# In the up pass, the gate groups of two tiles are run together, three in a row, behind the second tile

## The reference

```python
q  = (xt @ wq).reshape(t, 8, 2, 128)
s  = einsum('thpc,pnc->thpn', q, subkeys)      # 128 keys on each side
sv, si = top_k(s, 16)                          # 16 best on each side
cand   = sv[:, :, 0, :, None] + sv[:, :, 1, None, :]
cv, ci = top_k(cand, 16)                       # 16 of 256 pairs
eidx   = ia * 128 + ib                         # one of 16384 experts
gate   = softmax(cv)
hc  = gelu(einsum('chkd,cd->chk', u[eidx], x)) # up
out = einsum('chk,chkd->cd', hc * gate, v[eidx]) # down
```

## Time and profile before

| | |
|---|---|
| median of 3 runs | 3200.64 us (3191.85 to 3200.99) |
| the profiled execution | 3202.49 us, of which the span is 3200.7 us |
| PE busy | 3069.8 us, 96% of the span |
| DVE, POOL, ACT busy | 2551.4, 1746.1, 1382.4 us |
| DMA | 920.92 MB, mean 288 GB/s |
| matmuls of the up tiles (L1637), both layers | 6144 records |
| matmuls of the gate groups (L1669) | 1536 records, 192 groups |
| matmuls of the down pass (L1689) | 4608 records |

### The profile page before, as it was taken

The page is one execution under the profiler, slowest core; times in us unless marked ns, Lnnn a source line. Parts: engine busy times, 40 slices in busy tenths (PEclk is TensorE's granted clock), DMA queues, the critical chain, the costliest instruction groups (busy, mean ns, idle before and its releaser), DMA issues.

```text
span 3200.7 us, 46734 instructions
## 1 busy us (share of the span) xinstructions
PE 3069.8 (96%) x17222; PEld 2780.8 (87%) x17222; DVE 2551.4 (80%) x4953; ACT 1382.4 (43%) x2559; POOL 1746.1 (55%) x1160
## 2 busy tenths in 40 slices
PE   7879999999999999999888889999999999999997
PEld 7879999999998888888685789999999988888886
DVE  7755999977775999999567358989877759999987
ACT  2522343477764333333344223343777653333332
POOL 4543488887775444443130223788877755544442
PEclk9989999999999999999887899999999999999998
DMA  3212499999999999999130022799999999999993
GB/s 106 77 53 91 128 340 337 339 397 393 393 392 373 401 400 399 401 397 351 53 95 1 27 67 80 274 348 342 371 400 387 395 370 394 399 401 400 398 400 138
DMA packets 286579, 920.92 MB, mean 288 GB/s; under 512 B 27344, under 2 KB 77392, under 8 KB 282688
## 3 DMA queue, kind: packets, MB, share of 16 engines
q1 hardware_dynamic: 154336, 415.63, 35.9%
q0 software_dynamic: 111280, 404.77, 33.4%
q10 hardware_dynamic: 20736, 97.53, 7.4%
HBM read 817.34 MB, written 102.38 MB: 287 GB/s over the span
## 4 chain that ended last, share of the span: by engine, by line
PE 77%; DVE 16%; DMA 3%; POOL 2%; issue 1%; ACT 1%; DVEq 0%; ACTq 0%; SPq 0%
PE ps L1689 34%; PE ps L1637 22%; PE ps L1563 11%; PE ps L1669 5%; POOL low L604 2%; DMA raw<-uT 1%; PE ps L1811 1%; DVE xn L948 1%; DVE xl L941 1%; DVE cand L1218 1%; DVE cand L1225 1%; DVE slot L1231 1%; PE ps L1765 1%; PE ps L1800 1%; DVE rowsB L1129 1%
## 5 line engine op out<-in xcount | busy, mean ns | idle before, releaser
L762 ACT ACTIVATE high<-raw 128x1024 fp32r<-128x1024 f32 x512 | 542.7, 1060 | 992.2 <-PE ps L1689 665.9
L1637 PE MATMUL ps<-xh,high 128*128 128x384 f32 x2048 | 699.1, 341 | 14.8 <-POOL low L604 14.6
L604 POOL TENSOR_TENSOR low<-raw,high 128x1024 fp32r<-128x1024 f32 x256 | 614.2, 2399 | 167.2 <-ACT high L762 160.5
L1637 PE MATMUL ps<-xh,low 128*128 128x384 f32 x2048 | 687.4, 336 | 0.0
L1637 PE MATMUL ps<-xl,high 128*128 128x384 f32 x2048 | 686.2, 335 | 0.0
L1689 PE MATMUL ps<-high,hh 128*128 128x512 f32 x1536 | 483.5, 395 | 7.9 <-DVE low L1301 7.9
L1689 PE MATMUL ps<-low,hh 128*128 128x512 f32 x1536 | 481.1, 394 | 0.0
L1689 PE MATMUL ps<-high,hl 128*128 128x512 f32 x1536 | 480.3, 393 | 0.0
L595 POOL DMA_INDIRECT rowsA<-v,pick x192 | 271.3, 1413 | 296.9 <-DVE ps L1136 288.8
L1637 PEld LDWEIGHTS ps<-xh,high 128*128 128x128 f32 x2048 | 386.1, 189 | 20.8 <-POOL low L604 19.8
L595 POOL DMA_INDIRECT rowsB<-v,pick x192 | 240.2, 1251 | 271.0 <-DVE ps L1136 255.6
(11 more groups left out here) (279 smaller groups left out, 5043.5 us busy)
## 6 DMA issues: line engine op xcount, KB each, us to landing
raw<-uT SPq DMA_DIRECT2D x256, 512.0 KB
raw<-v SPq DMA_DIRECT2D x256, 512.0 KB
gate_dram<-gblk ACTq DMA_DIRECT2D x24, 2048.0 KB
gt<-gate_dram SPq DMA_DIRECT2D x32, 1536.0 KB
s_dram<-sring ACTq DMA_DIRECT2D x120, 384.0 KB
sring<-s_dram SPq DMA_DIRECT2D x120, 384.0 KB
raw<-wts SPq DMA_DIRECT2D x74, 512.0 KB, 3.6
rowsB<-u,pick POOLq DMA_INDIRECT x192
```

The costliest lines, as they stand in the source:

```text
L604: pool.tensor_tensor(low[:, m % 4], raw[:, m % 4], high[:, (m + 2) % 3].bitcast(F32), ALU.subtract).then_inc(sem("lo_ready"), 1)
L762: act.activation(high[:, (m + 2) % 3], tile_raw(m), ACT.Copy).then_inc(sem("hi_ready"), 1)
L1637: ins = pe.matmul(ps[:, m % 2, 0:DN], w[:, c], x[:, c, 0:DN], start=(c == 0 and k == 0), stop=(c == NC - 1 and k == 2))
```

## The change

`groups_of` gives nothing for an even tile, and for an odd tile m what the old one gave for m-1 and m together.

```diff
 def groups_of(m):
 
-    lo = min(int(max(0, m - GROUP0) * GROUPS_PER_TILE), DN // 4)
+    if m % 2 == 0:
+        m -= 1
+        lo = hi = min(int(max(0, m + 1 - GROUP0) * GROUPS_PER_TILE), DN // 4)
+        return range(lo, hi)
+    lo = min(int(max(0, m - 1 - GROUP0) * GROUPS_PER_TILE), DN // 4)
     hi = min(int(max(0, m + 1 - GROUP0) * GROUPS_PER_TILE), DN // 4)
     return range(lo, hi)
```

## The result

The changed kernel takes 3236.2 us (median of 4, 3231.01 to 3240.3) beside 3200.81 before: ratio 1.0109 (95% interval 1.0088 to 1.013), 35 us slower. Timed once more, it was 1.0103 (1.0085 to 1.0121). Forecast were +14 us and at most 3232. The direction was right, and the pause of PE at the third group is there; but it is larger than I made it, and something that I had put "under cover" costs 9 us beside the 17 of the pause.

The account below looks back on a forecast made before the run. PE was taken to set the pace. Bank pause 10.5 + ACT's small gelu and slot copy 1 + uT loads 1.5 + late store 1 - switches 0 = +14 us, giving 3214.5 us, range 3198 to 3232.

Parts of the forecast that it names:

- under cover: POOL's low halves and gathers, DVE's one-hots and SP's loads in the gate stretch: shifted but hidden, 0 us.
- what is removed: One switch between tile and groups and back per pair, 32 a layer: at most 0.01 us each, taken as 0.
- The bound of 5 us: Most that saved switches could give, if the slower first matmul step after a group (0.25 against 0.17) were a price.
- The pause: PE waits before each row's third group for ScalarE's copy to free the bank: 0.17 us a row, 10.5 us total.
- The rule of the Trainium skill: Rotate groups through banks; by it alone a group (0.89) outlasts a copy (0.58), so two banks lose nothing.
- the 1.5 us for them: ACT's waits for uT loads reaching the next row: perhaps three a layer by 0.3 us, 1.5 to 2 us.
- the 1 us for tiles 64 and 68: Small gelu and slot copy in front of high_tile at m = 64 and 68: 0.5 us a layer, 1 us.
- Rival 2: ACT's lateness from uT loads runs from row to row and reaches PE: 3240 us, chance 0.12.
- The sign of being wrong that I had named: No idle time before third groups, or idle in front of a tile ended by POOL, or PE waiting for weighed one-hots.
- Moved at the end: The last 2 MB store leaves one iteration later, behind high_tile(126): 0.5 us a layer, 1 us, ends 0 and 5.
- Rival 4: The clock falls in the gate stretches; one in ten of 128 tiles at half clock gives 3255 us, chance 0.02.
- Rival 3: Faster: a switch between tile and first group has a hidden price; 0.2 us without a pause gives 3188, chance 0.06.

Follow-up runs that it names:

- third_bank: The changed kernel, but from tile 69 to 117 the third group of a row has its own PSUM bank: 3216.63 us, ratio 1.0047 to the kernel before.
- copy_first: The changed kernel with ScalarE's weighings in their old iterations and the group copies put in front of them: 3221.87 us, ratio 1.0064 to the kernel before.
- ring28: The changed kernel with a ring of seven groups of one-hots in place of six (HOTS = 28): 3222.16 us, ratio 1.0062 to the kernel before.
- gather_cap: The changed kernel, but up to m = 121 GpSimd issues no gather beyond the layer's 200th: 3226.02 us, ratio 1.0074 to the kernel before.
- mended: The changed kernel with old order from tile 118, a third bank from tile 69 to 117, ring of seven: 3202.43 us, ratio 1.0000 to the kernel before.

## Why the prediction was wrong

**What bounds the kernel; what is removed.** Right. The switch was put at 0 with at most 0.01 a switch, and was worth 0.013. The bound of 5 us from the 0.25 against 0.17 us after a switch was no gain at all.

**The pause.** The mechanism was right and shown by third_bank. The schedule held: copy from 1.08 after the odd tile's end (measured 1.09), done at 1.66 (1.67), the third group's turn without a wait at 1.62 (its matmuls were due at 890.52, 1.62 after 888.90). What was mis-sized is "0.17 a row": it measured 0.27. I took POOL's release of PE, matmul 0.06 after the end; after ACT's copy the weights follow after 0.11 and the matmul after 0.14 (890.57 to 890.71). That is 0.19 late; the rest of the 0.27, 0.08, is the restart. 62 rows make 16.8 us in place of 10.5. copy_first splits it into ACT's order and the copy itself, about half each; the forecast had ACT as the later one by 0.2, which agrees.

The rule of the Trainium skill that I had weighed ("Perfetto Trace Analysis", section "Matmuls") agrees with third_bank once the number of banks is that of the row. That a copy (0.58) is shorter than a group (0.89) was no sufficient test: what must fit under the other group is the wait for the own group's end, the copy and the two releases.

**Moved on ACT.** The uT loads made no extra trouble: over the windows of the earlier trace rows ACT's waits for them fell from 21.2 to 14.5 us in layer 0 and from 29.5 to 15.9 in layer 1, and the pairs of the steady stretch are all alike (11.27 to 11.32 in layer 0). So the 1.5 us for them came to nothing. So did most of the 1 us for tiles 64 and 68: the pair from tile 64 takes no more than its neighbours, and the pair from tile 68 takes 11.66 in place of 11.35, 0.04 over the pause. Rival 2, lateness that runs from row to row, gave nearly the measured time (3240) but is wrong as a cause; the pairs would differ from one another.

**Under cover.** This is the step that failed: "DVE gets its ring slots back in bunches of three ... the ring of six groups is two rows deep, so the one-hots are ready a row ahead", and "two gathers in front (2.5) ... thin, but hidden". I had counted time on DVE and on GpSimd, and not followed who stands behind whom at the last groups. The one-hots were in time for PE, as I said; but behind the last of them, in DVE's order, stood the products with v, behind those in GpSimd's queue the gathers, and behind the gathers the low half of tile 121. It cost 20.23 - 15.54 = 4.7 us a layer (the changed kernel against ring28), 9.4 in all, where I had 0. By the starts of tiles 120, 121 and 122, 3.2 of the 4.7 are PE's stop, 7.42 against 4.25, and 1.5 the lower clock after it, 8.56 against 7.03 (tile 121 itself is 1.8 longer, but the row behind it takes 2.80 in place of 2.94). gather_cap and ring28 each remove both, at two different links of the chain. The sign of being wrong that I had named, an idle time in front of a tile ended by POOL, is what the profile shows.

The same chain stands at the start of the groups, behind tiles 61, 63 and 65, in both layers: the first group of a row frees the ring, DVE makes one-hots and two products with rows of u, GpSimd a gather and the low half, and PE waits. One turn in layer 0 (start, us, what):

```profile
651.05 0.91 PE ps L1673 x8
...
651.97 0.69 DVE hotA L1276
652.67 0.60 DVE hotB L1276
653.26 1.15 DVE rowsB L1133 x2
...
654.67 0.95 POOL rowsB L599
...
655.64 2.41 POOL low L608
...
658.10 4.44 PE ps L1641 x24
```

The three pairs there take about 11.5 us each (one of the twelve 11.36), 0.46 over 11.03 in place of the 0.27 of the pause. That is 0.6 us a layer more, 1.2 in all, and with the ring of seven most of it goes (11.27, 11.44, 11.30).

**Moved at the end.** Right in size, as far as can be told. From tile 123 to the down pass the seven profiles with the late store average 27.05 over their two layers, the seven others 25.52; of these 1.53 us, 0.91 is group 95 itself, which now stands in this stretch. That leaves 0.6 us a layer for the late store, forecast 0.5; but the single values of each kind spread over 2 us and more, so the 0.6 is uncertain by about as much, and no run moves the store alone.

**The sum.** 16.8 for the pauses, 9.4 for the queue at tile 121 with the clock behind it, 1.2 for the same chain at the start, 1.2 for the store: 28.6 of the 31 to 35 us measured (31 by the medians of the second comparison, 35 by the first). Against the forecast of 14, the pause was short by 6.3, the queue by 10.6, and the 2.5 for ACT didn't come. What is left of the time stands in tiles 0 to 62, where the executions of one and the same kernel differ by more than that; whether the change costs anything there stays open.

**The clock.** Rival 4 was not the cause, but it was not absent: after the pauses of 0.2 us the granted clock stayed at 1.00 for the whole steady stretch, as I argued; after the stop of 3 us in front of tile 121, which I had put at nothing, it fell, and that makes 1.5 us a layer of the 4.7. Rival 3, a hidden price of the switch, is out by mended: 0.013 us.

## What to carry to other kernels

When work is bunched, count the buffers against the longest run of the bunch, and lay out on paper not only how long the consumer's copy takes but when that engine gets to it: here two banks cost 0.27 us a row, and half of that was the order of ScalarE's own work. Then follow each ring that gets its slots back later, not to the engine that fills it but through everything that stands behind it in that engine's order and in the next queue: the dearest single wait of this change was a gather in GpSimd's queue, several links away from the group that had moved, and a third of its price was paid only after it, at the lower clock. And where two profiles differ in a stretch that the change doesn't touch, that difference is what chance can do there; compare stretches that repeat to the digit.

## What the runs showed of the hardware

PE's busy time hides short pauses: 2.4% of the steady stretch was lost (11.30 for 11.03) while the windows gave 99.70 of 100 us busy, since each record of a group's matmul (about 0.27: eight of them span 1.05 in the earlier trace rows at a pace of 0.11) is longer than its share of the pace; the idle time in front of the weight loads (0.19) and the time from start to start showed it. ACT's copy let PE's weights go after 0.11 us (890.57 to 890.68), POOL's subtraction after 0.05 (2621.49 to 2621.54 in the kernel before).

Pauses of 0.2 us, one every 11.3 us, left the granted clock at 1.00, and so did the stop of 1.29 us in the kernel before. At the end of each of the ten stops of 2.5 to 3.2 us in front of tile 121 (five profiles, two layers) the clock fell to its lower level, each time for about 3.4 us (in layer 0 of the changed kernel from 978.5 to 981.9), in which the matmuls of a tile followed one another after 0.32 us in place of 0.17.

And switching PE between the float32r matmuls of a tile and the float32 ones of a group cost 0.013 us, less than can be seen in one record.
